# Attention steps of a fused two-layer block reordered: PSUM evacuation before the softmax sums and weights, transposes three half slots later

## The reference

```python
p_c = masked_softmax(jnp.einsum('bqghd,bngd->bghqn', qb, k_cmp), valid_c)      # compressed keys
o_c = jnp.einsum('bghqn,bngd->bqghd', p_c, v_cmp)
p_s = masked_softmax(s_s, valid_s)                                             # selected blocks
p_w = masked_softmax(jnp.einsum('bqghd,bkgd->bghqk', qb, kwb), valid_w)        # window
return gb[..., 0, None] * o_c + gb[..., 1, None] * o_s + gb[..., 2, None] * o_w
```

## Time and profile before

| what | value |
|---|---|
| median of three runs | 2407.16 us (2400.61 to 2407.31) |
| profiled execution | 2402.47 us, span 2400.9 us |
| mean granted TensorE clock | 0.966 |
| busy: TensorE, VectorE, ScalarE, GpSimd | 94%, 66%, 46%, 6% |
| DMA | 420.62 MB, mean 175 GB/s |
| chain that ended last | TensorE 81%, VectorE 12%, ScalarE 5% |

### The profile page before, as it was taken

The page is one execution under the profiler, slowest core; times in us unless marked ns, Lnnn a source line. Parts: engine busy times, 40 slices in busy tenths (PEclk is TensorE's granted clock), DMA queues, the critical chain, the costliest instruction groups (busy, mean ns, idle before and its releaser), DMA issues.

```text
span 2400.9 us, 40751 instructions
## 1 busy us (share of the span) xinstructions
PE 2245.3 (94%) x15128; PEld 1915.5 (80%) x15128; DVE 1575.2 (66%) x2358; ACT 1096.2 (46%) x1724; POOL 132.7 (6%) x128
## 2 busy tenths in 40 slices
PE   3679999999999999989999998999999999999997
PEld 3678887777777778878988777888888888888886
DVE  6868767666666558676465666766566566566766
ACT  2234454444444356444445345444444444445554
POOL 0001000000000000020000000200000000000303
PEclk7889999999999999999799999999999999999998
DMA  8979733333333346644443333555555555555552
GB/s 331 343 284 346 273 123 124 123 132 109 121 124 123 124 165 224 232 142 147 153 132 124 124 123 126 172 178 186 189 186 187 190 183 188 188 184 187 171 167 79
DMA packets 114685, 420.62 MB, mean 175 GB/s; under 512 B 13089, under 2 KB 13217, under 8 KB 114305
## 3 DMA queue, kind: packets, MB, share of 16 engines
q1 hardware_dynamic: 106848, 390.68, 47.8%
q0 software_dynamic: 7712, 28.19, 3.4%
HBM read 412.52 MB, written 6.29 MB: 174 GB/s over the span
## 4 chain that ended last, share of the span: by engine, by line
PE 81%; DVE 12%; ACT 5%; issue 1%; DMA 0%; DVEq 0%; SPq 0%; ACTq 0%
PE ps L1943 44%; PE ps L1944 22%; PE ps L2031 5%; DVE acc L1188 3%; PE ps L2235 2%; DVE wlo L1157 2%; ACT whi L662 2%; PE ps L2236 1%; ACT pr L974 1%; DVE wlo L1212 1%; PE ps L2370 1%; DVE acts L1168 1%; PE ps L2285 1%; PE ps L2002 0%; DVE mx L1686 0%
## 5 line engine op out<-in xcount | busy, mean ns | idle before, releaser
L1943 PE MATMUL ps<-acts,whi 128*128 128x512 f32 x3520 | 1299.6, 410 | 34.4 <-DVE nsb L1163 13.7
L1157 DVE TENSOR_TENSOR wlo<-raw,whi 128x1024 fp32r<-128x1024 f32 x647 | 816.0, 1270 | 697.8 <-ACT whi L662 696.4
L662 ACT ACTIVATE whi<-raw 128x1024 fp32r<-128x1024 f32 x671 | 704.5, 1059 | 881.8 <-PE ps L1944 773.0
L1944 PE MATMUL ps<-acts,wlo 128*128 128x256 f32 x3520 | 992.5, 282 | 0.0
L1943 PEld LDWEIGHTS ps<-acts,whi 128*128 128x128 f32 x3520 | 669.3, 190 | 211.2 <-issue 19.2
L1944 PEld LDWEIGHTS ps<-acts,wlo 128*128 128x128 f32 x3520 | 672.9, 191 | 4.4 <-issue 3.4
L1943 PE MATMUL ps<-hidn,whi 128*128 128x512 f32 x1280 | 450.4, 394 | 6.6 <-DVE s L1163 6.0
L1944 PE MATMUL ps<-hidn,wlo 128*128 128x256 f32 x1280 | 361.3, 282 | 0.0
L1943 PEld LDWEIGHTS ps<-hidn,whi 128*128 128x128 f32 x1280 | 240.9, 188 | 63.2 <-DVE wlo L1157 5.2
L1944 PEld LDWEIGHTS ps<-hidn,wlo 128*128 128x128 f32 x1280 | 242.6, 190 | 0.5 <-issue 0.5
L662 ACT ACTIVATE half<-ps 128x256 f32<-128x256 f32 x353 | 132.1, 382 | 88.9 <-PE ps L1944 75.8
(11 more groups left out here) (317 smaller groups left out, 1962.4 us busy)
## 6 DMA issues: line engine op xcount, KB each, us to landing
raw<-in_stream SPq DMA_DIRECT2D x735, 512.0 KB, 4.0
graw<-in_ada_gate POOLq DMA_DIRECT2D x32, 512.0 KB, 5.6
gate_dram<-stage POOLq DMA_DIRECT2D x32, 128.0 KB, 2.2
gab<-gate_dram POOLq DMA_DIRECT2D x8, 512.0 KB, 5.1
xt<-in_x SPq DMA_DIRECT2D x1, 2048.0 KB, 9.4
xt<-in_x POOLq DMA_DIRECT2D x1, 2048.0 KB, 9.1
out<-y__143 SPq DMA_DIRECT2D x4, 512.0 KB, 2.8
con<-in_con SPq DMA_DIRECT2D x1, 898.0 KB, 4.9
```

What stands on the lines that cost most here:

```text
L662: return nc.scalar.activation(dst, src, ACT.Copy)
L1157: tt(wlo[:, n % SPLIT, :], raw[:, g % RAW, :], whi[:, n % SPLIT, :].bitcast(F32), ALU.subtract).then_inc(raw_used, 1)
L1943: mm(ps[bank + n][:, :], whi[:, n0 % SPLIT, c:c + P], act[:, off + kt + k, :], start=kt + k == 0, stop=False)
L1944: ins = mm(ps[bank + n][:, 0:T], wlo[:, n0 % SPLIT, c:c + P], act[:, off + kt + k, 0:T], start=False, stop=kt + k == last)
```

## The change

On VectorE, in groups 0 to 2, split 7 and the boundary come ahead of `sums` and `weighted(1)`, and the splits behind them are numbered one on, so that 13 of them lie inside `attention`. On ScalarE split 5 comes ahead of the first half's exponentials (in all four groups), and in groups 0 to 2 split 10 comes ahead of the copies of transposed weights. On TensorE the steps of k = 17 to 22 come at k = 20 to 25 in groups 0 to 2 and stay where they were in group 3. In the output projection the evacuation of block 0's last part comes ahead of `no_split(1)` on both engines.

```diff
--- before.py
+++ after.py
@@ -1000,27 +1000,31 @@
                 t(4)
                 act.wait_ge(s.v_ps, g + 1)
                 copy(vtm[:, :, :], four(7)).then_inc(s.vtm_done, 1)
+                t(5)
                 act.wait_ge(s.m0_done, g + 1)
                 for j in range(HPG):
                     exps(g, 0, j)
-                t(5)
                 act.wait_ge(s.cd_done, g + 1)
                 nc.scalar.activation(pc[:, :, :], pc[:, :, :], ACT.Exp, scale=DH ** -0.5).then_inc(s.cexp_done, 1)
                 t(6)
                 t(7)
-                boundary()
+                if boundary is not None:
+                    boundary()
                 t(8)
                 t(9)
+                late = 0 if boundary is None else 1
+                if late:
+                    t(10)
                 for n in (0, 2):
                     act.wait_ge(s.p1_ps, 4 * g + n + 1)
                     copy(pt[:, n, :], ps[4 + n][:, :]).then_inc(s.pt_act, 1)
                 cmp_weights(g, 1)
-                t(10)
+                t(10 + late)
                 out_hi(g, 1)
                 act.wait_ge(s.p0_ps, 2 * g + 1)
                 copy(pt[:, 0, :], ps[5][:, :]).then_inc(s.pt_act, 1)
                 cmp_weights(g, 0)
-                t(11)
+                t(11 + late)
                 out_hi(g, 0)
 
             for g in range(3):
@@ -1030,7 +1034,7 @@
                     tile(t0 + j)
 
                 attention(g, here, lambda: halves(t0 + 7))
-                for j in range(12, 16):
+                for j in range(13, 16):
                     here(j)
                 halves(t0 + 15)
 
@@ -1048,14 +1052,14 @@
                 if j == 5:
                     halves(N0 + 5)
 
-            attention(3, here, lambda: None)
+            attention(3, here, None)
             here(12)
             here(13)
             halves(N0 + 13)
             here(14)
             here(15)
+            halves(N0 + 15)
             no_split(1)
-            halves(N0 + 15)
             for b in (2, 3):
                 for j in range(8):
                     here(8 * b + j)
@@ -1756,21 +1760,24 @@
                 cmp_scores(g)
                 t(5)
                 t(6)
+                late = 0 if boundary is None else 1
+                if late:
+                    t(7)
+                    boundary()
                 sums(g)
                 weighted(1)
-                t(7)
-                boundary()
+                t(7 + late)
                 weighted(0)
-                t(8)
-                t(9)
+                t(8 + late)
+                t(9 + late)
                 for n in (1, 3):
                     dve.wait_ge(s.p1_ps, 4 * g + n + 1)
                     nc.vector.tensor_copy(pt[:, n, :], ps[4 + n][:, :]).then_inc(s.pt_dve, 1)
-                t(10)
+                t(10 + late)
                 out_lo(g, 1)
                 dve.wait_ge(s.p0_ps, 2 * g + 2)
                 nc.vector.tensor_copy(pt[:, 1, :], ps[6][:, :]).then_inc(s.pt_dve, 1)
-                t(11)
+                t(11 + late)
                 out_lo(g, 0)
 
             for g in range(3):
@@ -1813,14 +1820,15 @@
                 if j == 5:
                     residual(E, 0, s.part_done)
 
-            attention(3, here, lambda: None)
+            attention(3, here, None)
             here(12)
             here(13)
             residual(E + 4, 1, s.res_done)
             here(14)
             here(15)
+            dve.wait_ge(s.res_done, 4)
+            residual(E + 8, 0, s.res_done)
             no_split(1)
-            residual(E + 8, 0, s.res_done)
             for b in (2, 3):
                 for j in range(8):
                     here(8 * b + j)
@@ -2371,6 +2379,7 @@
                 mm(dst, vcmp[:, g, :], pt[:, 4, :], start=False, stop=True).then_inc(s.o_ps, 1)
 
             def attention(g, k):
+                late = 3 if g < 3 else 0
                 if k == 2:
                     scores1(g, 0)
                     scores1(g, 1)
@@ -2381,19 +2390,19 @@
                     scores0(g)
                 if k == 7:
                     cmp_scores(g)
-                if k == 17:
+                if k == 17 + late:
                     turned1(g, 0)
                     turned1(g, 1)
-                if k == 18:
+                if k == 18 + late:
                     turned1(g, 2)
                     turned1(g, 3)
-                if k == 19:
+                if k == 19 + late:
                     turned_cmp(g)
                     turned0(g, 0)
                     turned0(g, 1)
-                if k == 20:
+                if k == 20 + late:
                     outputs(g, 1)
-                if k == 22:
+                if k == 22 + late:
                     outputs(g, 0)
 
             for g in range(3):
```

## The result

The changed kernel takes 2380.6 us (median of four runs, 2379.9 to 2382.7) against 2405.7 for the kernel before in its four; the ratio is 0.990, 95% interval 0.988 to 0.992. That is faster by 1.0%, and 1.4 us under the forecast of 2382. The profiled execution took 2380.6, against 2379.9 by the sum.

A forecast was written before the change was run, and what follows sets the result against it. TensorE, busy 94% of the span, bounds the kernel, so only its waits and slow stretches can be won. Savings of 18.6 + 2.7 + 1.3 = 22.6 us from a mean of 2404.4 give 2382, range 2375 to 2394.

The forecast's parts named there:

- The place and its cause: Boundaries of groups 0 to 2: TensorE waits 13.7 us for the first `nsb` sum, because of VectorE's order.
- Groups 0 to 2: Evacuation ahead of sums and weights, with later transposes, saves 18.6 us: 20.1 less hand-overs and new waits.
- The slow stretches: Low TensorE clock after the boundary waits of groups 0 to 2 costs 2.8, 1.8 and 1.8 us.
- the wait for the copies: New TensorE wait for the first copy of transposed weights, 0.4 us in each of groups 0 to 2.
- What is late next: After the boundary, weights come 0.9 us before the later transposes; left at 17, these would wait 3.3.
- Group 3: Split 5 and its half copies ahead of the exponentials: saves 3.85 less 1.15 for a later wait, 2.7 us.
- Tail: Output projection, block 0's residual ahead of `no_split(1)`: 1.6 us saved less a 0.3 wait for split 16, 1.3.
- The case with the gain at -1.2: Output projection: split 16 also stands behind a GpSimd instruction of 2.47 us, gain -1.2 instead of 1.3.
- (a): Rival: the clock falls again at the new waits in the groups, costing 7.0 us, time 2389; chance 0.10.
- (b): Rival: the wait only moves, `turned1` waiting for weights, about 2400; with the change not working, chance 0.07 together.
- (c): Rival: VectorE's 6.75 us stretch from boundary to weights runs stretched; at factor 2.5, 2415, slower; chance 0.03.
- The level: Starting time of the kernel before, taken as 2404.4 us, the mean of its four executions.

The follow-up runs named there:

- x10: Kernel before with only the transposes of groups 0 to 2 three half slots later; the same kernel's timed run gave 2405.0 against 2404.4, ratio 1.000.
- x7: Changed kernel with transposes of groups 0 to 2 back at half slot 17 and split 10 behind the copies, consistently on all three engines: 2395.1 us, ratio 0.996.
- x4: Kernel before with five unused fp32 matmuls filling TensorE's wait behind half slot 15 of groups 0 to 2: 2398.6 us, ratio 0.998.
- x9: Kernel before with two unused fp32 matmuls behind half slot 15, so TensorE stands 2.6 us at the boundary: 2405.8 us in one execution.
- x2: Changed kernel with TensorE's transposes in groups 0 to 2 one half slot later than before instead of three: 2394.1 us, ratio 0.995.
- x1: Changed kernel with the transposes of groups 0 to 2 back at half slot 17 on TensorE only: 2420.7 us, 1.006 of the kernel before.

## Why the prediction was right, point by point

**The place and its cause.** Right: "The wait is order on VectorE, not lack of data" is shown by the pair x10 and x7, which split the change: with the old order the wait for `nsb` is 13.1 us, with the new one there is none. The cost of leaving out the shift, worked out in the same way before x7 ran, was put at 15.3 us over the changed kernel; the stages give 14.8 and the medians 14.5.

**Groups 0 to 2**, 18.6 forecast and 17.9 measured. Two sizes were off. The slow stretches cost 5.6 by x4, not 6.4. The term that was mis-sized is the full-speed time of the two half slots behind a restart: 2 x 1.40 = 2.8 was taken from half slots in the middle of a stream, but in x4, at clock 1.00, the same way from restart to transposes takes 3.06 by the chain (1321.17 to 1324.23). The same error is in the way to the late transposes: five half slots with the restart took 7.30 (1312.47 to 1319.77), not 7.0. Against that the wait for the copies came to about 0.8 over three groups and not 1.2. With these three put right the sum is 13.7 + 5.6 - 0.3 - 0.8 = 18.2; the last 0.3 stay open. The signs named beforehand for single groups (6.9, 5.9, 5.9 shorter) came out at 6.6, 5.7 and 5.6.

**What is late next.** Right in place: the weights were ready 1.1 us before TensorE came, where 0.9 was forecast, and the prediction's 3.3 for transposes left at 17 was measured in x7.

**Group 3**, 2.7 forecast and 2.55 measured: 1.0 of standing at the first sum as said, then, by TensorE's weight loads, 0.6 for the weights (0.4 was said) and 1.0 for the copy (1.15). **Tail**, 1.3 and 1.3, with 5.46 us for the updates where 5.2 was said, and a wait of 0.2 for a split behind them where 0.3 was said. The case with the gain at -1.2, in which split 16 stands behind GpSimd as well, did not arise: GpSimd was done 0.6 us before that split began.

**The rivals.** (a), a clock that falls at the new waits, did not come about: none of them is over 1.0 us. But the argument against it, "2.4 us of standing left it at 1.00", was weak: at the same place, behind tile 15, the same 2.4 us were followed by the low clock in x4 and x9, whose edits do not touch it (granted clock 0.50 from 1491.3 to 1494.3 in x4), and x2 lost the clock after 1.8. One row was taken for a rule; no new wait was long enough to put it to the test. (b), the wait moving to the weights, is what happens without the shift; the shift is what prevents it. (c) had no part in the groups, where GpSimd is silent: VectorE's stretch from the boundary to the weights took 6.8 us (1311.91 to 1318.71) where 6.75 was counted. The stretched updates stayed in the tail.

**The level.** The choice of 2404.4 for the kernel before was near its later medians (2404.4 to 2405.7). The stages saved 0.9 us less than forecast and the medians 2.5 more, so that the forecast lies within 1.4 us of the median is partly luck; the same holds for the sum against the profiled execution (2379.9 for 2380.6), whose attention happened to begin 0.7 us sooner than in the kernel before.

## What to carry to other kernels

Where one engine stands for another that is not short of time, find the two pieces of work whose order makes it wait, and then compute who wants the piece that went back and when: here, in groups 0 to 2, 14.6 of the 17.9 us hung on moving that consumer, though moving it alone gave 0.3. An order written out on three engines is one object; x1 changed it on two of them and not on the third, and was slower than no change at all. And price a stall with the slow clock that may follow it, here 5.6 us on top of 13.7.

## What the runs showed of the hardware

**The clock after a wait.** In the 13 profiled executions, between 1215 and 1620 us, TensorE stood, and then: 1.0 us or less, clock held, each time; 1.8, fell in two of six (x2: fell twice, held once; x1, at another place: held three times); 2.3 to 2.5, fell in 12 of 13 at the start of the feed-forward network, in 2 of 13 some 18.6 us after that, in 2 of 5 behind tile 15 of the output projection, and in all three before the outputs of x1; 2.6 (x9), fell in two of three; 3.2 and more, fell in all 17. Behind the restart it ran at 1.2 GHz for about 3 to 6 us. Between the ends the same kernel at the same wait does both, and the place counts beside the length: 12 of 13 and 2 of 13 are for almost the same wait. What makes the difference is not shown. The Trainium skill, "TensorE: Matmul & The Clock Gate", "Part 1: The HAM clock gate", says that the number of matmuls that run at the low rate before the full one is granted differs between runs of one kernel. The trace agrees, and shows it between groups of one execution: after the same 4.6 us of standing, the low clock lasted to 5.6 us behind the restart in group 0 of the kernel before and to 4.2 in group 1.

**The short transposes run at the full clock.** "Part 4: PE-mode transpose" of the same page of the Trainium skill says that full rate does not engage for transposes. The trace does not agree: the eight at 1319.77 and the eight at 1322.04, among other matmuls, take 0.87 us in a stretch at clock 1.00, against 1.97 in x7 (1255.19) at a clock of 0.50.

**VectorE beside GpSimd.** Four updates took 5.46 us beside a square and an addition on GpSimd and 1.66 alone; two splits took 4.05 beside the same square and 2.35 alone. GpSimd's square took 2.08 beside the updates and 2.81 beside the splits. By how much each is slowed goes with the partner and not only with the overlap.
